# Rotary permutation of query and key blocks: a shuffle on VectorE in the place of a permutation matmul

## What is computed

```python
def partial_rope(x, cos, sin):
    half = ROT_DIM // 2                      # 8
    ...
    x1 = x[..., :half]
    x2 = x[..., half:ROT_DIM]
    rot = jnp.concatenate([x1 * c - x2 * s, x2 * c + x1 * s], axis=-1)
    return jnp.concatenate([rot, x[..., ROT_DIM:]], axis=-1)
...
dq = partial_rope(dq.reshape(B, S, DIFF_HEADS, 2, DIFF_HEAD_DIM), cos, sin)
dk = partial_rope(dk.reshape(B, S, DIFF_HEADS, 2, DIFF_HEAD_DIM), cos, sin)
...
mq = partial_rope(mq.reshape(B, S, MOBA_HEADS, MOBA_HEAD_DIM), cos, sin)
mk = partial_rope(mk.reshape(B, S, MOBA_HEADS, MOBA_HEAD_DIM), cos, sin)
```

## Time and profile before

| | |
|---|---|
| median of 3 runs | 1243.81 us (1243.55 to 1246.93) |
| span of the profiled execution, first to last instruction | 1243.2 us |
| mean granted clock of TensorE | 0.992 |
| PE busy | 1198.1 us (96%), 8800 matmuls |
| DVE busy | 889.3 us (72%) |
| ACT busy | 768.2 us (62%) |
| POOL busy | 567.3 us (46%) |
| DMA | 249.84 MB, mean 201 GB/s |

### The profile page before, as it was taken

The page is one execution under the profiler, slowest core; times in us unless marked ns, Lnnn a source line. Parts: engine busy times, 40 slices in busy tenths (PEclk is TensorE's granted clock), DMA queues, the critical chain, the costliest instruction groups (busy, mean ns, idle before and its releaser), DMA issues.

```text
span 1243.2 us, 27547 instructions
## 1 busy us (share of the span) xinstructions
PE 1198.1 (96%) x8800; PEld 1103.0 (89%) x8800; DVE 889.3 (72%) x1833; ACT 768.2 (62%) x1730; POOL 567.3 (46%) x505
## 2 busy tenths in 40 slices
PE   8999999988897999999999999999999999999997
PEld 8989988988887999999999999999888888888885
DVE  5776768889575839992688888860576767686766
ACT  5446676465665555557777788875555555555554
POOL 3664543435464348988877777778200000000000
PEclk9999999999999999999999999999999999999999
DMA  6668656538633445555576666668676576767663
GB/s 236 226 204 301 226 200 198 168 117 311 237 120 119 136 135 172 184 179 177 189 216 207 203 200 214 200 209 272 196 245 210 190 256 188 256 195 257 189 198 103
DMA packets 85826, 249.84 MB, mean 201 GB/s; under 512 B 8019, under 2 KB 29692, under 8 KB 84988
## 3 DMA queue, kind: packets, MB, share of 16 engines
q1 hardware_dynamic: 77356, 209.62, 53.2%
q0 software_dynamic: 8400, 39.34, 8.5%
HBM read 237.38 MB, written 13.12 MB: 202 GB/s over the span
## 4 chain that ended last, share of the span: by engine, by line
PE 84%; DVE 7%; ACT 4%; issue 3%; DMA 2%; POOL 1%; DVEq 0%; ACTq 0%; SPq 0%; POOLq 0%
PE psum L684 83%; DMA ring<-v_rows 2%; ACT w_hi L1171 1%; DVE s_sb L1751 1%; DVE w_lo L1737 1%; DVE arena L1790 1%; PE psum L883 0%; DVE rstd L1731 0%; ACT arena L1328 0%; ACT arena L1154 0%; DVE arena L1946 0%; DVE xres L1871 0%; POOL arena L1650 0%; DVE arena L1852 0%; ACT L1328 0%
## 5 line engine op out<-in xcount | busy, mean ns | idle before, releaser
L1567 POOL TENSOR_TENSOR w_lo<-ring,w_hi 128x512 fp32r<-128x512 f32 x368 | 492.1, 1348 | 277.2 <-ACT w_hi L1171 266.5
L1171 ACT ACTIVATE w_hi<-ring 128x512 fp32r<-128x512 f32 x734 | 445.2, 627 | 274.7 <-PE psum L684 263.8
L684 PE MATMUL psum<-h_hi,w_hi 128*128 128x256 f32 x1832 | 534.5, 292 | 21.8 <-DVE w_lo L1737 7.4
L684 PE MATMUL psum<-h_lo,w_hi 128*128 128x256 f32 x1832 | 520.8, 284 | 0.0
L684 PE MATMUL psum<-h_hi,w_lo 128*128 128x256 f32 x1832 | 520.3, 284 | 0.0
L684 PEld LDWEIGHTS psum<-h_hi,w_hi 128*128 128x128 f32 x1832 | 353.2, 193 | 36.1 <-issue 23.1
L684 PEld LDWEIGHTS psum<-h_lo,w_hi 128*128 128x128 f32 x1832 | 353.6, 193 | 0.3
L684 PEld LDWEIGHTS psum<-h_hi,w_lo 128*128 128x128 f32 x1832 | 353.3, 193 | 0.0
L1737 DVE TENSOR_TENSOR w_lo<-ring,w_hi 128x512 fp32r<-128x512 f32 x238 | 188.6, 793 | 130.7 <-ACT w_hi L1171 130.1
L684 PE MATMUL psum<-w_hi,h_hi 128*128 128x512 f32 (+1 forms) x592 | 224.2, 379 | 4.4 <-ACT w_hi L1171 1.8
L684 PE MATMUL psum<-w_hi,h_lo 128*128 128x512 f32 (+1 forms) x592 | 222.2, 375 | 0.0
(11 more groups left out here) (214 smaller groups left out, 1126.5 us busy)
## 6 DMA issues: line engine op xcount, KB each, us to landing
ring<-u_t SPq DMA_DIRECT2D x128, 512.0 KB, 3.6
ring<-v_rows SPq DMA_DIRECT2D x128, 512.0 KB, 3.6
ring<-weights SPq DMA_DIRECT2D x115, 512.0 KB, 4.1
arena<-mods POOLq DMA_DIRECT2D x48, 512.0 KB, 5.5
routing_weights<-s_sb SPq DMA_DIRECT2D x32, 320.0 KB, 4.2
s_sb<-routing_weights POOLq DMA_DIRECT2D x5, 2048.0 KB, 10.3
bias_rows<-bias_row POOLq DMA_DIRECT2D x1, 1536.0 KB, 11.4
xres<-x_t SPq DMA_DIRECT2D x2, 512.0 KB, 4.6
```

Source lines behind the costliest of these rows:

```text
L684: return nc.tensor.matmul(out, lhs, rhs, start=start, stop=stop, **kw)
L1171: nc.scalar.activation(w_hi[:, half, :], src, ACT.Copy).then_inc(hi_done, 1)
L1567: nc.gpsimd.tensor_tensor(w_lo[:, half, :], src, w_hi[:, half, :].bitcast(F32), ALU.subtract)\
```

## The change

The permutation is done by DVE: a `stream_shuffle`, in which each group of 32 partitions is reordered by the same list of 32 indices, PARTNER, reads RAW + b and writes the tile SIG + b. The rotated pairs (d, d + 8) of a head lie within its first 16 partitions, so within the first of its two groups of 32. The list is the same for all groups, so that in the second group of a head too the first 16 partitions are swapped; there the sine is 0. The multiplication by the sine then reads that tile in place of the PSUM bank. PE's `rope_turn`, the list `pending`, the banks of `vbuf` that it filled, and the matrix `perm` with its load are gone. DVE waits for `cos_done` before the shuffle, and for its own steps by the new semaphore `rope_step`. The place of the rotation in DVE's order stays.

```diff
--- before.py
+++ after.py
@@ -151,6 +151,7 @@
 
 
 QUADS = T // 4
+PARTNER = [d ^ 8 if d < 16 else d for d in range(32)]
 COPY_LAG = 4
 GRP = 16
 GROUPS = P // GRP
@@ -167,7 +168,7 @@
 NPAR = _at
 CST = {}
 _at = 0
-for _name, _w in (("ident", P), ("perm", P), ("cos", T), ("sin", T), ("mask", TRI), ("iota", P),
+for _name, _w in (("ident", P), ("cos", T), ("sin", T), ("mask", TRI), ("iota", P),
                   ("valid", TT), ("rev", TRI)):
     CST[_name] = (_at, _at + _w)
     _at += _w
@@ -241,7 +242,6 @@
         cos_t, sin_t = blk(TAB), blk(TAB + 1)
         mask = flat(MSK, 2)[:, 0:TRI]
         rel_c = flat(REL, 2)[:, 0:TRI]
-        perm = flat(MSK, 2)[:, TRI:TRI + P]
         sheet = flat(SHEET, 8).rearrange("p (h j) -> p h j", h=HEADS)
         cbias = flat(CBIAS, 2).rearrange("p (i h n) -> p i h n", i=TT, h=HEADS)
         csc = flat(CSC, 2).rearrange("p (i g c) -> p i g c", i=TT, g=2)
@@ -373,6 +373,7 @@
         h_ready = sem("h_ready")
         cos_done = sem("cos_done")
         sin_done = sem("sin_done")
+        rope_step = sem("rope_step")
         rope_done = sem("rope_done")
         scores_done = sem("scores_done")
         max_done = sem("max_done")
@@ -449,8 +450,6 @@
                 a_order += [s + (j,) for j in range(TT)]
             elif k == "proj":
                 a_order += [s]
-                if s[1] in FIRST1:
-                    v_order += [("rope", s[1])]
             elif k in ("pv", "gates"):
                 a_order += [s]
             elif k == "subln":
@@ -598,7 +597,7 @@
             load_slot(1)
             sp.dma_start(par[:, :], params).then_inc(par_in, 16)
             for name, dst in (("ident", ident[:, :]), ("iota", iota[:, :]), ("valid", valid[:, :]),
-                              ("cos", cos_t), ("sin", sin_t), ("mask", mask), ("perm", perm)):
+                              ("cos", cos_t), ("sin", sin_t), ("mask", mask)):
                 sp.dma_start(dst, consts[:, CST[name][0]:CST[name][1]]).then_inc(small_in, 16)
             sp.dma_start(rel_c[0:33, :], consts[0:33, CST["rev"][0]:CST["rev"][1]]).then_inc(small_in, 16)
             for n in range(2, RING):
@@ -690,7 +689,7 @@
                     return
                 n = filled_a + 1
                 pe_.wait_ge(const_set, 1)
-                pe_.wait_ge(small_in, 16 * 8)
+                pe_.wait_ge(small_in, 16 * 7)
                 pe_.wait_ge(a_read, n - 1)
                 for _ in range(count):
                     mm(psum[:, n % 2, 0:P], ones[:, :], ident[:, :], True, True)
@@ -769,19 +768,11 @@
             def part_ready(kind):
                 return lambda c: pe_.wait_ge(part_lo, PART_BASE[kind] + c + 1)
 
-            def rope_turn(b):
-
-                pe_.wait_ge(small_in, 16 * 8)
-                pe_.wait_ge(a_read, filled("proj", rope_blocks[b]))
-                out = take_v(VT[("rope", rope_blocks[b])])
-                mm(out, perm, blk(RAW + b), True, True).then_inc(v_done, 1)
-
-            pending = []
             for s in STEPS:
                 kind = s[0]
                 fill_wait(FILLERS.get(s, 0))
                 if kind == "small":
-                    pe_.wait_ge(small_in, 16 * 8)
+                    pe_.wait_ge(small_in, 16 * 7)
                     pe_.wait_ge(par_in, 16)
 
                     rel = par[0:33, PAR["rel"][0]:PAR["rel"][1]]
@@ -811,9 +802,6 @@
                     for x in range(2 * slots):
                         half = half_ready(k0 + x // 2, x % 2)
                         for j in range(jobs):
-                            if x == 0 and j == 2:
-                                while pending:
-                                    rope_turn(pending.pop(0))
                             if x == 0:
                                 out[j] = take(at[s + (j,)])
                             i, col = (j // 2, (j % 2) * T) if jobs == 4 else (j, 0)
@@ -835,10 +823,6 @@
                         split_pair(AT[s], SPLIT[SLOT_AT[s]], lambda c, base=base: pe_.wait_ge(h_ready, base + c + 1))
                     elif s[1] not in ("dq1", "nq1"):
                         split_projection(AT[s], SPLIT[SLOT_AT[s]], lambda c, base=base: pe_.wait_ge(h_ready, base + c + 1))
-                    if s[1] in rope_blocks:
-                        pending.append(rope_blocks.index(s[1]))
-                        if len(pending) > 1:
-                            rope_turn(pending.pop(0))
                 elif kind == "gates":
 
                     pe_.wait_ge(a_read, filled("proj", "gt"))
@@ -1624,7 +1606,7 @@
                         load_mod(m)
                 elif kind == "proj" and s[1] in rope_blocks:
                     b = rope_blocks.index(s[1])
-                    pool.wait_ge(small_in, 16 * 8)
+                    pool.wait_ge(small_in, 16 * 7)
                     pool.wait_ge(a_read, filled(*s))
                     nc.gpsimd.tensor_tensor(blk(QK + b), blk(RAW + b), cos_t, ALU.mult).then_inc(cos_done, 1)
                     if s[1] == "mq0":
@@ -1753,13 +1735,13 @@
 
             def rope(b):
 
-                n = VT[("rope", rope_blocks[b])]
-                dve.wait_ge(v_done, n + 1)
-                tmp = blk(SIG + b)
-                v.tensor_tensor(tmp, vbuf(n), sin_t, ALU.mult).then_inc(v_read, 1)
-                dve.wait_ge(v_read, n + 1)
+                turned = blk(SIG + b)
                 dve.wait_ge(cos_done, b + 1)
-                v.tensor_tensor(blk(QK + b), blk(QK + b), tmp, ALU.add).then_inc(rope_done, 1)
+                v.stream_shuffle(turned, blk(RAW + b), PARTNER).then_inc(rope_step, 1)
+                dve.wait_ge(rope_step, 2 * b + 1)
+                v.tensor_tensor(turned, turned, sin_t, ALU.mult).then_inc(rope_step, 1)
+                dve.wait_ge(rope_step, 2 * b + 2)
+                v.tensor_tensor(blk(QK + b), blk(QK + b), turned, ALU.add).then_inc(rope_done, 1)
 
             v.memset(ones[:, :], 1.0).then_inc(const_set, 1)
             v.memset(eps_c[:, 0:1], EPS)
@@ -2311,15 +2293,10 @@
     inv = np.float32(500000.0) ** (-np.arange(0, 16, 2, dtype=np.float32) / np.float32(16))
     ang = np.arange(T, dtype=np.float32)[:, None] * inv[None, :]
     cos, sin = np.ones((P, T), np.float32), np.zeros((P, T), np.float32)
-    swap = np.eye(P, dtype=np.float32)
     for base in (0, DH):
         for d in range(8):
             cos[base + d] = cos[base + 8 + d] = np.cos(ang[:, d])
             sin[base + d], sin[base + 8 + d] = -np.sin(ang[:, d]), np.sin(ang[:, d])
-            a, b = base + d, base + 8 + d
-            swap[a, a] = swap[b, b] = 0
-            swap[a, b] = swap[b, a] = 1
-    put("perm", swap)
     put("cos", cos)
     put("sin", sin)
     q, k = np.arange(P)[:, None], np.arange(T)[None, :]
```

## The result

The changed kernel takes 1248.68 us (median of 6 runs, 1247.37 to 1250.75), the kernel before 1244.68 beside it (6 runs, 1243.55 to 1246.93). The ratio is 1.0032, with a 95% interval from 1.0020 to 1.0043: 4 us slower. The forecast was 1242.9, from 1238.0 to 1246.4, so it had the wrong sign and the time lies outside its range. Timed once more together with the last experiments, the same kernel gave 1.0042 (1.0027 to 1.0057).

A forecast was written before the change was run, and what follows sets the result against it. The prediction took TensorE's matmuls as the bound, with DVE and POOL nearly as full. Six places summed to -0.95 us; 1243.2-0.95+0.6 (profiled span to median) gave 1242.9 us, range 1238.0 to 1246.4.

The forecast's parts named there:

- given to the rival: In plain blocks, PE waiting for w_lo was claimed only by the slower rival, chance 0.12.
- The start: dq0 to dq3: DVE's w_lo for dq3 comes later, PE starts dq3 at 26.2 and ends at 29.1: +0.7 us.
- the two permutations in ACT's stretch around the Silu: End of dq3 to 32.84: ACT sets the pace, so two removed permutations change nothing: 0.
- the rival that it comes through: Places of the rotations: DVE finds its turns and PE's saving is realized, -5.7 us, 1238.1 us; chance 0.25.
- the sum of held times: One block: mutually exclusive DVE and POOL work takes 2.9 us with the multiplication, where PE alone wants 2.86.
- a plain run of blocks can just keep up with PE: Plain blocks: with turns in the listed order, the next w_lo ends at t+2.9, against PE's 2.86 us.
- the slower rival: Blocks with a POOL DMA issue: late addition waits for issue and w_lo; four cases, 5.5 us, 1249 us; chance 0.12.
- the addition that comes too late: Mechanism of the slower rival: DVE's addition falls behind POOL's issue and w_lo, PE stands 1.6 us; chance 0.12.
- the pair of rotations: Ahead of w_lo of dv's second slot: DVE has two rotations in a row, 5.0 us instead of 4.7.
- place 3: 32.84 to 47.61, dk1 to dk3 and dv's first two halves: two rotations precede a w_lo, +0.3 us.
- place 4: 59.44 to 77.57, mq1 to the start of mk2: four blocks at 2.9 instead of 3.3, then mod 4: -1.55 us.
- The rival of a dear shuffle: Every rotation: the shuffle costs much more than a pass; at 0.84 us each, 1245 us; chance 0.05.

The follow-up runs named there:

- e3_pe_matmuls_kept: The changed kernel plus a matmul of the permutation's size, into an unread bank, at each old place of the permutation: 1249.20 us, ratio 1.0040.
- e5_before_sbuf_input: The kernel before, with only the sine multiplication reading the unpermuted block in SBUF instead of the PSUM bank: 1249.14 us, ratio 1.0037.
- e4_no_shuffle: The changed kernel without the shuffle, the multiplication reading the unpermuted block: 1247.79 us, ratio 1.0025.
- e7_issue_first: The changed kernel with POOL's DMA issue for the modulation rows moved ahead of its wait for the block: 1252.83 us, ratio 1.0071.
- e2_both_from_psum: The changed kernel with shuffle and multiplication both writing a free PSUM bank, so multiplication and addition read PSUM: 1239.21 us, ratio 0.9956; again 1239.08, 0.9960.

## Why the prediction was wrong

**Right.** The mechanism was the one of the forecast: DVE with two inputs in SBUF and POOL work by turns, the multiplication had been outside of this and came inside, and w_lo became what PE waits for: ahead of dq3, of dv's and mv's third half and of mk2 as forecast, but in plain blocks too (up to 37.85 and 76.73), which I had given to the rival. The shuffle's size was right (0.44 for 0.42), the mask's load is 0.01 us. The start was right: dq3 began at 25.98 for 26.2, and ended at 29.1 as forecast; the two permutations in ACT's stretch around the Silu brought nothing. That PE's saving would mostly fall into waits was right; the rival that it comes through is out (the changed kernel is slower, and e3_pe_matmuls_kept has 1.0040).

**The step that failed** is the assumption, in the sum of held times, that "a plain run of blocks can just keep up with PE", with DVE and POOL taking turns in the best order: POOL's w_lo, multiplication, cosine, addition, DVE's w_lo. A resource booked for 2.9 of 2.86 us has no place for a lost turn, and turns were lost: the addition or w_lo falls behind POOL's issue and POOL's w_lo, 1.4 to 1.6 us at once. I had that as the slower rival, "the addition that comes too late", with 0.12, four cases and 1249 us. It came about in four cases, in two of them with w_lo in the addition's place. That its time fits too (1248.7) is in part luck: it had the four cases at 6.5 us together, and here places 3 and 4 came out 2.9 us above the forecast, part of it by the pair of rotations below, and the clock, which wasn't in it, put in 1.5. Its row of before (44.80, 2.04 us in the earlier trace rows) was as good an evidence as the one with which I set it aside (66.78). I ought to have asked what a turn hangs on: at 67.36 w_lo passed behind a cosine of 0.75 us, and in e5_before_sbuf_input, with the cosine held up to 0.94, it lost its turn at the same distance to the issue.

**The term that was mis-sized** is place 3, dk1 to dv: +0.3 forecast, +2.6 measured (17.4 for 14.8). w_lo of dk2 took 2.23 instead of 0.68 (35.36), the addition behind it 1.84 (38.50), and the two rotations in a row ahead of dv's second slot took 1.45 and 1.38 for multiplication and addition of the second (47.19, 48.68), each behind a w_lo of POOL's. Of place 4 a third was lost by the same (74.27, 77.38): -1.0 for -1.55.

**What wasn't in it:** a wait of PE of over 2.3 us can bring its clock down to 1.2 GHz for some 3.4 us afterwards, 1.5 us more. Before, PE's longest wait for w_lo in this stretch was 1.4 us and its clock 1.00 throughout. But the trace of before has the case further on, and the forecast doesn't use it: there PE waits 3.42 us for w_lo, up to 388.38, and then its matmuls follow at 0.21 us with a granted clock of 0.50 until 391.3. As the forecast itself had a wait of 2.5 us ahead of dq3 (23.7 to 26.2), that row bore on it.

**The rival of a dear shuffle** is out: the shuffle took 0.44 us, and without it the kernel is still slower than before (e4_no_shuffle, 1.0025).

## What to carry to other kernels

Before moving an operation to VectorE, look at where its inputs will lie: here a multiplication with one input in PSUM was never held up (0.41 to 0.43 us in each of the sixteen cases, in the kernel before and with the shuffle into PSUM), and the same with both in SBUF cost 0.77 and the kernel 4.5 us, beside a busy GpSimd. A scratch tile in a free PSUM bank took the same three passes from 1.0032 to 0.9956. And when the sum of what excludes each other comes to the pace of the bound engine, forecast by what a lost turn costs, not by the best order.

## What I had not expected of the hardware

- Whether DVE or POOL gets the turn went with how long POOL's cosine had taken just before: at 0.25 to 0.27 us behind an issue, w_lo took 0.68 us behind a cosine of 0.74 to 0.77 us, and 2.2 to 2.4 us behind one of 0.82 to 0.99, sixteen times each.
- A DMA issue of POOL can be part of what DVE waits for: an addition with two SBUF inputs that came during it waited for it and for all that POOL had behind it (2.54 us in e7_issue_first, with cosine and w_lo). The Trainium skill (SBUF — State Buffer, "Who interferes with whom") infers that a `tensor_tensor` wouldn't contend with descriptor generation. Where nothing of POOL's followed the issue at once, the trace agrees (0.42 and 0.68 us, at 40.22 and 74.12 of the same run); where SBUF reads of POOL's followed at once, DVE could lose the time of the issue too.
- Loading the mask of the shuffle takes 0.01 us in the profile, and a shuffle of 128x256 numbers 0.44 us into SBUF and 0.42 into PSUM.
- The same wait of PE (2.39 and 2.41 us, ahead of dq3) was followed by the full clock in one execution and by 0.59 for 4.2 us in another. The changed kernel's times scatter more (1247.2 to 1254.6 in its second timing) than those of e2_both_from_psum (1236.8 to 1240.7 over both of its timings). The clock isn't shown to be the reason: the execution of 1254.6 us has a mean granted clock of 0.992, as those of 1249.5 and 1249.7 have.
